# Expert rows by index lists made on TensorE, with unused places out of range

## The reference, cut to what matters

```python
N_GROUPS, EXPERTS_PER_GROUP, TOP_K_IN_GROUP, D_EXPERT = 4, 8, 2, 256
...
    p_top, g_idx = lax.top_k(p_grp, 1)                 # one of 4 groups
...
    w_top, e_idx = lax.top_k(p_e, TOP_K_IN_GROUP)      # two of its 8 experts
    w_top = w_top / jnp.sum(w_top, axis=-1, keepdims=True) * p_top
...
    hidden = jax.nn.silu(jnp.einsum("bld,edf->blef", h, lp["w_exp_gate"])) * jnp.einsum(
        "bld,edf->blef", h, lp["w_exp_up"])
    hidden = hidden * gates.astype(h.dtype)[..., None]
    return jnp.einsum("blef,efd->bld", hidden, lp["w_exp_down"])
```

## Time and profile before

| | us |
|---|---|
| Median of 3 runs (lowest, highest) | 2629.16 (2627.85, 2636.6) |
| Profiled execution, its own time | 2629.61 |
| Its span | 2627.7 |
| PE busy in the span | 2209.9 (84%) |
| DVE, ACT, POOL busy | 1068.0, 508.5, 373.2 |

### The profile page before, as it was taken

How to read it: one execution, slowest core, us unless ns; L and a number is a source line. 1 busy time by engine, 2 the same in 40 slices (tenths; PEclk the granted TensorE clock), 3 DMA queues, 4 the chain that set the end, 5 groups by cost and what they waited for, 6 DMA issues and landing times. The chain is left out here.

```text
span 2627.7 us, 27002 instructions
## 1 busy us (share of the span) xinstructions
PE 2209.9 (84%) x9907; PEld 1374.1 (52%) x9907; DVE 1068.0 (41%) x1914; ACT 508.5 (19%) x1185; POOL 373.2 (14%) x379
## 2 busy tenths in 40 slices
PE   4789889899897989898898988889999795598980
PEld 2454555455544757667585776745555444343430
DVE  3574564665743454553535545410000056111116
ACT  0121211212202323323232332300000000111111
POOL 0041051230411011010201102000000000200005
PEclk9989989899898989899998989989999896799995
DMA  7011201101001010101101010043242295399973
GB/s 267 9 49 30 65 9 40 48 8 40 32 13 55 22 34 4 32 4 34 34 2 34 4 32 14 17 144 121 73 144 72 78 306 216 141 412 420 421 322 123
DMA packets 161406, 257.71 MB, mean 98 GB/s; under 512 B 11458, under 2 KB 127257, under 8 KB 147009
## 3 DMA queue, kind: packets, MB, share of 16 engines
q1 hardware_dynamic: 150905, 221.52, 24.0%
q10 hardware_dynamic: 5512, 18.56, 1.8%
q0 software_dynamic: 4928, 16.79, 1.7%
HBM read 229.26 MB, written 27.58 MB: 98 GB/s over the span
## 5 line engine op out<-in xcount | busy, mean ns | idle before, releaser
L642 PE MATMUL bank<-hT,shared 128*128 128x512 f32 x512 | 252.9, 629 | 13.3 <-DMA negm<-in_levels_dram 8.5
L1132 PE MATMUL bank<-hT,shared 128*128 128x512 f32 x384 | 175.4, 611 | 2.9 <-ACT spadded L1271 1.6
L1974 PE MATMUL bank<-ring,xgT 128*64 128x512 f32 (+1 forms) x416 | 151.6, 634 | 25.4 <-DMA ring<-in_w_exp_up_dram 13.0
L988 DVE TENSOR_TENSOR conv<-bank,negm 128x512 f32<-128x512 f32 x144 | 82.3, 599 | 184.4 <-PE bank L655 184.4
L642 PEld LDWEIGHTS bank<-hT,shared 128*128 128x128 f32 x512 | 94.7, 201 | 96.8 <-issue 88.1
L1212 PE MATMUL bank<-shared,hT 128*128 128x512 f32 x320 | 139.9, 592 | 0.0
L655 PE MATMUL bank<-D_,MT 128*128 128x128 f32 x960 | 125.4, 279 | 0.0
L1585 DVE SCALAR_TENSOR_TENSOR prod<-gth,bank 128x512 f32<-128x512 f32 x16 | 11.0, 687 | 272.7 <-PE bank L1559 272.7
L663 PE MATMUL bank<-DT,conv 128*128 128x128 f32 x960 | 121.6, 275 | 0.0
L1132 PEld LDWEIGHTS bank<-hT,shared 128*128 128x128 f32 x384 | 73.9, 197 | 89.7 <-issue 85.9
L1194 PEld LDWEIGHTS bank<-xT,M 128*128 128x128 f32 x640 | 88.4, 218 | 54.6 <-issue 41.3
(11 more groups left out here) (394 smaller groups left out, 3557.7 us busy)
## 6 DMA issues: line engine op xcount, KB each, us to landing
shared<-in_w_in_dram SPq DMA_DIRECT2D x58, 512.0 KB, 6.3
ring<-in_w_exp_gate_dram SPq DMA_DIRECT2D x26, 1024.0 KB, 18.1
ring<-in_w_exp_up_dram SPq DMA_DIRECT2D x26, 1024.0 KB, 20.4
ring<-in_w_exp_down_dram SPq DMA_DIRECT2D x26, 1024.0 KB, 15.4
aw<-in_w_ada_dram SPq DMA_DIRECT2D x8, 2048.0 KB, 7.5
yd<-ysb ACTq DMA_DIRECT2D x22, 512.0 KB, 8.3
aw<-in_w_ada_dram SPq DMA_DIRECT2D x8, 1024.0 KB, 21.5
shared<-in_w_in_dram SPq DMA_DIRECT2D x4, 2048.0 KB, 7.6
```

The costliest lines, as they stand in the source:

```text
L642: last = pe.matmul(bank[a][:, :], w4[:, n, k, :], hT[:, k, SEQ:T], start=(k == 0), stop=(k == KD - 1), skip_group_check=True)
L988: TT(out=X[:, u0:u0 + n, :], in0=bank[XB[g]][:, 0:n * P].rearrange("p (u n) -> p u n", n=P), in1=m, op=ALU.mult).then_inc(s["g_Xkept"], 1)
L1132: pe.matmul(bank[a][:, :], wn(n)[:, k, :], hT[:, k, SEQ:T], start=(k == 0), stop=(k == KD - 1))
L1974: last = pe.matmul(bank[2 + slot][at, :], xgT[:, slot, k, at], wgu[w][:, k, :, :], start=(k == 0), stop=(k == KD - 1))
```

## The change

- The lists are made on chip. DVE finds the row (`rowf`) and the place in the row (`inrow`) of each pair and makes two sets of comparison matrices, `at_place` (128 x 128) and `of_row` (128 x 22, times the token's number plus one); PE multiplies them, ten matmuls summed in one bank. A sum of zero marks an unused place.
- `idx` gets 2^20 more for an unused place. The gathers have `bounds_check` with `oob_is_err=False`: an index out of range is left out. `xg` is set to zero once, so that the rows not gathered hold finite values.
- Gathers of passes 0 and 1 are issued at the end of `route`, on POOL; the copy to `idxs` is gone.
- Results are stored by POOL's indirect DMA with destinations `dest`, out of range for unused places; ACT's plain stores are gone. All 4032 rows of `yd` are set to zero at the start of `merge`, by ACT's queue, in place of 1216 rows in `route`.
- The scatter to `lists`, still needed by the overflow loop, moves behind the gather of pass 3 in `experts`.
- Several small tiles now lie in others (`g1`, `sc2`, `rtmp`, `ring`), and DVE waits in tile 1 of `route` for the zeros of `lists`.

```diff
@@ merge
+                act.wait_ge(zero_ready, 1)
+                act.dma_start(yd.rearrange("(p b) (c n) -> p (b c) n", p=SLOT, c=4),
+                              zero[0:SLOT, :].unsqueeze(1).broadcast_to([SLOT, NPLACE // SLOT * 4, D // 4])).then_inc(yz_out, 16)
...
+                act.wait_ge(yz_out, 16)
@@ route
-                sp.dma_start(lists.rearrange("(p n) a -> p (n a)", p=SLOT), zero[0:SLOT, 0:NPLACE // SLOT]).then_inc(z_out, 16)
-
-                sp.dma_start(yd[NP * P:NPLACE, :].rearrange("(p b) (c n) -> p (b c) n", p=SLOT, c=4), zero[0:SLOT, :].unsqueeze(1).broadcast_to([SLOT, NMORE * 4, D // 4])).then_inc(yz_out, 16)
+                sp.dma_start(lists[NP * P:NPLACE, :].rearrange("(p n) a -> p (n a)", p=SLOT), zero[0:SLOT, 0:NMORE]).then_inc(z_out, 16)
...
-                sp.wait_ge(scattered, 16 * 2 * NT)
-                sp.dma_start(rows_[:, :], lists[0:NP * P, :].rearrange("(e n) a -> e (n a)", e=NP)).then_inc(rows_in, 16)
...
-                pe.wait_ge(rows_in, 16)
-                pe.transpose(bank[4][:, 0:NP], rows_[:, :], C(C_ID)[0:NP, 0:NP]).then_inc(rows_turned, 1)
+                pe.wait_ge(placed, 2)
+                for a in range(2 * NT):
+                    last = pe.matmul(bank[4][:, 0:NP], at_place[:, a, :], of_row[:, a, :], start=(a == 0), stop=(a == 2 * NT - 1))
+                last.then_inc(listed, 1)
...
+                pool.wait_ge(h2_out[0], 16 * 3)
+                pool.wait_ge(h2_out[1], 16 * 2)
+                for p in range(2):
+                    pool.wait_ge(taken, 1)
+                    pool.wait_ge(xg_blank, 1)
+                    pool.indirect_dma_start(out=xg[:, p, :], out_offset=None, in_=h2d,
+                                            in_offset=bass.IndirectOffsetOnAxis(ap=idx[:, LISTED[p]:LISTED[p] + 1], axis=0),
+                                            bounds_check=T - 1, oob_is_err=False).then_inc(got[p], 16)
...
+                dve.wait_ge(listed, 1)
+                empty = spare[:, 0:NP]
+                st.link(TS(out=empty, in0=bank[4][:, 0:NP], scalar1=0.0, scalar2=float(NOWHERE), op0=ALU.is_equal, op1=ALU.mult))
+                STT(out=idx[:, :], in0=bank[4][:, 0:NP], scalar=-1.0, in1=empty, op0=ALU.add, op1=ALU.add).then_inc(taken, 1)
+                st.link(STT(out=empty, in0=ends[:, 0:NP], scalar=cols[:, S_TOK:S_TOK + 1], in1=empty, op0=ALU.add, op1=ALU.add))
+                st.link(TS(out=dest[:, :], in0=empty, scalar1=-float(P), scalar2=None, op0=ALU.add))
@@ experts
+                def store(p):
+                    pool.wait_ge(y_act, p + 1)
+                    pool.wait_ge(y_dve, p + 1)
+                    pool.indirect_dma_start(out=yd, out_offset=bass.IndirectOffsetOnAxis(ap=dest[:, LISTED[p]:LISTED[p] + 1], axis=0),
+                                            in_=ysb[:, p % 2, :], in_offset=None, bounds_check=NP * P - 1, oob_is_err=False).then_inc(y_out[p % 2], 16)
+
+                for p in range(2, NP + 4):
...
+                    if p >= 4:
+                        store(p - 4)
+                    if p == 3:
+                        for t in range(NT):
+                            for n in range(2):
+                                pool.indirect_dma_start(out=lists, out_offset=bass.IndirectOffsetOnAxis(ap=slots[:, t, n:n + 1], axis=0),
+                                                        in_=cols[:, S_TOK + t:S_TOK + t + 1], in_offset=None).then_inc(scattered, 16)
...
-                    act.wait_ge(y_act, p + 1)
-                    act.wait_ge(y_dve, p + 1)
-                    act.dma_start(yd[LISTED[p] * P:(LISTED[p] + 1) * P, :], ysb[:, p % 2, :]).then_inc(y_out[p % 2], 16)
```

More of the change, by code:

```diff
@@ L82 @@
 NSTEP = T // SLOT - 1
[L83 removed]
+S_ROW = S_STEP + NSTEP
+S_PLACE = S_ROW + NP
+NCOL = S_ROW
 def small_constants():
@@ L201, in build @@
                 stage(deltanet, bank, cst, C, hT, ST, cwT, vecT, half, shared, oT, levels, w_in, w_gdn_out, state_gdn, new_gdn)
-                stage(merge, bank, hT, oT, yT, mT, shared, cT, ada, w_ada, b_ada, w_in, w_gdn_out, w_ssd_out)
+                stage(merge, bank, yd, hT, oT, yT, mT, shared, cT, ada, w_ada, b_ada, w_in, w_gdn_out, w_ssd_out)
             x1d = nc.dram_tensor("x1d", [T, D], F32, kind="Internal").ap()
@@ L211, in build @@
                 order = sb("order", [P, NX], U32, tail)
+                xg = sb("xg", [P, 2, D], F32, tail)
+                idxs = sb("idxs", [P, 2], U32, tail)
+                got = [sem(f"e_got{n}") for n in range(2)]
+                dest = sb("dest", [P, NP], U32, tail)
                 EW = KD * 2 * FX + FX // P * D
@@ L227, in build @@
                 lb2 = sb("lb2", [P, D], F32, tail)
-                stage(experts, bank, C, idx, more, order, lists, h2d, yd, w_exp_gate, w_exp_up, w_exp_down, wgu, wdn,
+                stage(experts, bank, C, cols, slots, xg, idxs, got, dest, idx, more, order, lists, h2d, yd, w_exp_gate, w_exp_up, w_exp_down, wgu, wdn,
                       x1, g2, lg2, lb2, x1d, ada, ln2_g, ln2_b)
-                stage(combine, half, slots, wts, yd, x1, g2, lg2, lb2, y_prompt, y_sample)
+                stage(combine, ring, half, slots, wts, yd, x1, g2, lg2, lb2, y_prompt, y_sample)
 def condition(nc, sb, sem, bank, cst, C, cols, hT, cT, modT, cwT, vecT, half, shared, first_in, x_prompt, x_sample, c,
@@ L1777, in _ @@
                         pool.tensor_tensor(out=rs[:, n, t:t + 1], in0=ve[:, n, t:t + 1], in1=half[:, 0:1], op=ALU.pow).then_inc(rs_ready, 1)
-                pool.wait_ge(z_out, 16)
-                pool.wait_ge(slots_ready, 1)
-                for t in range(NT):
-                    for n in range(2):
-                        pool.indirect_dma_start(out=lists, out_offset=bass.IndirectOffsetOnAxis(ap=slots[:, t, n:n + 1], axis=0),
-                                                in_=cols[:, S_TOK + t:S_TOK + t + 1], in_offset=None).then_inc(scattered, 16)
-                pool.wait_ge(scattered, 16 * 2 * NT)
+                pool.wait_ge(h2_out[0], 16 * 3)
[6 more added lines that the diff above has]
+                                            bounds_check=T - 1, oob_is_err=False).then_inc(got[p], 16)
             @block.vector
@@ L1927, in load_expert, with experts @@
         eng.dma_start(to, one.rearrange("(p k) f -> p k f", p=P)).then_inc(signal, 16)
-def experts(nc, sb, sem, bank, C, idx, more, order, lists, h2d, yd, w_exp_gate, w_exp_up, w_exp_down, wgu, wdn,
+def experts(nc, sb, sem, bank, C, cols, slots, xg, idxs, got, dest, idx, more, order, lists, h2d, yd, w_exp_gate, w_exp_up, w_exp_down, wgu, wdn,
             x1, g2, lg2, lb2, x1d, ada, ln2_g, ln2_b):
@@ L2190, in experts, with combine @@
             block.vector(further(dve_body))
-def combine(nc, sb, sem, half, slots, wts, yd, x1, g2, lg, lb, y_prompt, y_sample):
+def combine(nc, sb, sem, ring, half, slots, wts, yd, x1, g2, lg, lb, y_prompt, y_sample):
     own = ExitStack()
```

93 lines of the change are left out of this document (57 added, 36 removed).

## The result

The changed kernel takes 2612.34 us (median of 5, 2610.42 to 2616.19) where the kernel before takes 2629.62 in the same comparison (2627.85 to 2636.6): a ratio of 0.9937 [0.9922, 0.9952], or 17.3 us less. The forecast was 33.5 less. The range, 2586 to 2621, holds the time, but only because it was drawn wide enough to take in the second and third rival: the forecast's own range ended at 2605. The largest term gave less than half of what it was sized at.

The account below looks back on a forecast made before the run. It took transfers to bound the rounds of `experts`, and a serial chain the end of `route`. Terms -22 - 11.8 - 2.7 + 1 + 2 = -33.5 us from 2629.61 gave 2596 us, own range 2586 to 2605, 8-in-10 range to 2621.

Parts of the forecast that it names:

- second rival: In experts, skipped places cost as much as sent rows, so the 22 us are lost: 2618 us; chance 14%.
- third rival: Skipped rows save only part, or bunch in single passes, or merge stalls 10 us: 2605 to 2614 us; chance 14%.
- The largest term: In experts, gathers and stores without the unused places: 22 us less.
- Rows moved: In experts, unused places cost no transfer: 22 us less (0 to 30), 17 of it in seven rounds, at 421 GB/s.
- the lead of the loads: Less transfer in the five passes ahead of the rounds lets weight loads run ahead: 2 us less.
- Its own signs: In experts, being right would show as rounds of 24.5 to 25 us and PE's weight waits around 10 us or less.
- The list: Between `slotf` and the first transposes, making the list by matmuls lets PE start 11.8 us earlier (7 to 13).
- The zeros leave the route: In route, DVE no longer waits for the `h2d` store held up by the zeros: 2.7 us less.
- The zeros in merge: In merge, the fill's packets take turns with the weights and delay `load(1, 1)`: PE stalls 0 to 3.5 us, taken as 2.
- first rival: In merge, the zeros hold SP's loads and PE waits 48 us in place of 2: 2642 us; chance 14%.
- The last store: At the end of experts, longer issue on POOL and landing than ACT's store: 1 us more (0 to 2.5).
- The moved scatters: In experts, ten scatters to `lists` ahead of pass 4's gather on POOL are free, with some 2 us to spare.

Follow-up runs that it names:

- e1_spread: The changed kernel with consecutive places four partitions apart and single experts using both halves of 64; 2600.79 us, 0.989 of the kernel before.
- e4_skip_rest: The changed kernel with all places of passes 2 to 21 and of all stores out of range, output invalid; 2583.25 us, 0.9827 of the kernel before.
- e7_last_by_act: The changed kernel with only the last pass's store issued by ScalarE as one plain DMA; 2608.12 us, 0.9914 of the kernel before.
- e9_spread_half: The changed kernel with consecutive places four partitions apart within their half, single experts still filling partitions 0 to 63 first; 2605.89 us, 0.9915 of before.
- e12_list_only_again: The changed kernel with no place skipped and stores as plain ScalarE DMAs, keeping the matmul list, moved scatters and moved zeros; 2619.5 us.

## Why the prediction was right or wrong

**Rows moved: -22 forecast, -8.7 measured.** This is the step that failed. The price was right in kind, since the rounds are bound by transfers before and after, and over all passes the bytes went as said. What failed is "at 421 GB/s": I divided all bytes by the rate of all 16 engines, as if what skipping leaves out came off each engine alike. It came off those with high partitions; by the counts the busiest kept 103 of 112 rows in the rounds, and the rate fell to 406 GB/s. A smaller error stands ahead of it: "45.5%" is the mean of all 22 passes. The first five hold 111 rows in 640 places and the rounds 1062 in 1792, so a round moved 10.54 MB and not 10.39. Of the 9 us that the rounds fell short of my 17, some 3 are these bytes and some 6 the rate.

By the prediction's own parts: seven rounds gave 7.9 us, where 17 and most of the 2 for the lead of the loads should have shown, and the last three passes 0.4 for 3; the first five gave 0.4, for which I had nothing. With the rows spread (`e1_spread`) the same parts give 15.4, 3.1 and 0.5, 19.0 in all. So the step would nearly have held for another placement. Its own signs failed too: rounds of 24.5 to 25 us (25.9), and waits for weights around 10 us (20.5). The third rival named rows that bunch, but in passes against passes, not in engines, so that its 2605 to 2614 holds the time is luck.

**The list: -11.8 forecast, -10.2 measured.** The chain was right to 0.1 us. Against it were that the first GpSimd DMA of the block took 1.89 us to issue and not 1.0, and that PE is let go by the second gather's landing at the block's end, not by the first's. That 2 of the 10.2 come from gathering fewer rows was not in the sum.

**The zeros leave the route: -2.7, measured -2.7,** and, put back, +2.2 (VectorE's wait 2.1). **The zeros in merge: +2, measured 0.0.** The estimate of packets in turns was too dear: it had the loads there at 1762 to 1770, and the last part of `load(1, 1)` landed at 1755.3. The first rival (SP's loads held until the zeros are through, 2642) did not happen: 16128 KB from ScalarE's queue and SyncE's loads ran together for 90 us, and the fill landed only at 1816.5. The three loads of `aw` that were issued beside it landed after 24.9, 15.0 and 11.3 us for 12.2, 7.6 and 7.3, within what PE could wait. The Trainium skill's words on a generator "locked for exclusive use" (Perfetto Trace Analysis, DMA Instruction - HWDGE) can't mean here that it is locked until a fill of 16 MB is through; whether a shorter lock is in the 9.69 us at the slab's issue, no run tells.

**The second rival** (a skipped place costs what a row costs, 2618) comes near the time and is wrong: `e4_skip_rest` keeps 128 places a transfer and its passes take 265.2 us.

**The last store: +1 (0 to 2.5), measured +3.6.** I priced issue and landing and left out the time that GpSimd is late behind its own DMA at the block's end. `e7_last_by_act` takes 3.2 us of it back.

**The moved scatters: 0, measured 0**: passes 0 to 4 took 70.8 us for 71.2.

## What to carry to other kernels

Before bytes that are left out are divided by the total rate, ask which partitions they come off: a transfer that all engines share ends with the engine that lost nothing. A mean rate that falls, or holes in its slices while the mean DMA share stays at 1.00, point to it; a permutation of places that costs next to nothing at run time (`e1_spread` adds seven small VectorE operations, `e9_spread_half` none) gives much of it back. Take the share of used places from the passes that are bound by transfers, not from all. And compare stages by their own anchors: `merge` and `route` repeated to 0.3 us from kernel to kernel, while the program ahead of them moved everything behind it by up to 10.

## What was not expected of the hardware

PE's first matmul of `merge` lay between 1714.98 and 1724.78 us in the profiled executions (`e9_spread_half` and `e12_list_only_again`), though the program ahead of it is all but the same in every kernel. That is more than the rows gave (8.7), and the medians carry some of it.

A place out of range in an indirect DMA still sends a small packet; 3584 of them in 162.5 us took 1.4% of the DMA engines' time. GpSimd is held at a block's end by its own late DMA, 7.5 us to its next operation, with or without data, where it is 5.5 us after a memset.

Left open: whether it is the DMA engine or the port of a partition's memory that was overloaded; each kernel here moves both together.
